# Layer 0's experts in fours, chosen and added by one-hot matmuls on the chip

## The reference

```python
for i in range(DEPTH):                      # 2 layers
    h = h + mixer_i(rmsnorm(h))             # attention, then chunked gMLP
    h = h + hier_moe(rmsnorm(h))            # 32 experts, 1024 -> 2 x 256 -> 1024
    h = h + sigmoid(rmsnorm(h) @ W_g) * (p[i] @ W_p)   # "ple"

h1 = einsum('td,edf->tef', t, w_gate); h2 = einsum('td,edf->tef', t, w_up)
a = silu(h1) * h2 * gates[:, :, None]       # gates: zero except 2 experts a token
y = einsum('tef,efd->td', a, w_down)
```

## Time and profile before

| what | us |
|---|---|
| median of 3 runs (lowest, highest) | 1098.43 (1094.73, 1100.7) |
| span of the profiled execution | 1095.3 |
| PE busy / DVE / ACT / POOL | 1021.0 / 352.3 / 186.5 / 124.5 |
| DMA, mean over the span | 281 GB/s, 308 MB |

### The profile page before, as it was taken

How to read it: one execution, slowest core, us unless ns; L and a number is a source line. 1 busy time by engine, 2 the same in 40 slices (tenths; PEclk the granted TensorE clock), 3 DMA queues, 4 the chain that set the end, 5 groups by cost and what they waited for, 6 DMA issues and landing times.

```text
span 1095.3 us, 13338 instructions
## 1 busy us (share of the span) xinstructions
PE 1021.0 (93%) x5092; PEld 603.9 (55%) x5092; DVE 352.3 (32%) x885; ACT 186.5 (17%) x384; POOL 124.5 (11%) x170
## 2 busy tenths in 40 slices
PE   6989999999998878999999999999999999988793
PEld 5766676444443324754457777777754444433372
DVE  4556225222222103632123444220342222221254
ACT  2123213111111112221012110000211111111221
POOL 2444001111111101000000000000021111110101
PEclk9999999899999999999999999999979999999997
DMA  9947885799999997933325223335469999999811
GB/s 360 369 142 245 360 349 193 296 419 418 418 419 420 419 418 302 389 145 154 154 108 196 86 110 116 115 141 230 159 248 420 418 417 418 418 419 422 321 60 43
DMA packets 61715, 308.12 MB, mean 281 GB/s; under 512 B 13778, under 2 KB 21266, under 8 KB 29650
## 3 DMA queue, kind: packets, MB, share of 16 engines
q1 hardware_dynamic: 44064, 273.53, 62.0%
q0 software_dynamic: 14656, 25.72, 7.0%
q10 hardware_dynamic: 2930, 7.99, 2.0%
HBM read 310.23 MB, written 21.08 MB: 302 GB/s over the span
## 4 chain that ended last, share of the span: by engine, by line
PE 66%; DMA 17%; issue 7%; DVE 3%; POOLq 3%; POOL 2%; ACT 1%; SPq 0%; ACTq 0%; DVEq 0%
PE ps L1574 14%; PE ps L1754 9%; PE ps L1795 9%; DMA scr_sb<-stream 8%; PE ps L1724 8%; PE ps L1583 7%; DMA ring_sb<-stream 5%; PE ps L1484 3%; PE ps L1526 3%; PE ps L1655 2%; PE ps L1560 2%; POOLq L510 2%; DMA scr_sb<-bs 1%; POOL ring_sb L511 1%; PE ps L1730 1%
## 5 line engine op out<-in xcount | busy, mean ns | idle before, releaser
L1574 PE MATMUL ps<-ring_sb,scr_sb 128*64 128x512 f32 x624 | 162.9, 611 | 14.9 <-DMA ring_sb<-stream 13.2
L1574 PEld LDWEIGHTS ps<-ring_sb,scr_sb 128*64 128x64 f32 x624 | 52.0, 141 | 119.6 <-issue 119.6
L1574 PE MATMUL ps<-scr_sb 128*64 128x512 f32 x320 | 108.6, 604 | 5.2 <-DMA scr_sb<-stream 5.2
L1583 PE MATMUL ps<-ring_sb,scr_sb 128*64 128x512 f32 x432 | 99.3, 597 | 1.1 <-ACT scr_sb L671 0.9
L1754 PE MATMUL ps<-hn_sb,ring_sb 128*128 128x288 f32 x384 | 97.9, 411 | 0.0
L1795 PE MATMUL ps<-scr_sb,ring_sb 128*128 128x288 f32 x384 | 95.2, 407 | 0.0
L1075 DVE SCALAR_TENSOR_TENSOR scr_sb<-ps,scr_sb 128x256 f32<-128x256 f32 x32 | 15.5, 484 | 243.1 <-ACT scr_sb L667 243.1
L1724 PE MATMUL ps<-ring_sb,hn_sb 128*128 128x512 f32 x192 | 83.3, 593 | 0.0
L1795 PEld LDWEIGHTS ps<-scr_sb,ring_sb 128*128 128x128 f32 x384 | 72.2, 190 | 19.3
L1754 PEld LDWEIGHTS ps<-hn_sb,ring_sb 128*128 128x128 f32 x384 | 71.5, 190 | 19.3 <-issue 0.4
L1655 PE MATMUL ps<-scr_sb,ring_sb 128*128 128x288 f32 x256 | 64.3, 406 | 0.0
(11 more groups left out here) (288 smaller groups left out, 1246.6 us busy)
## 6 DMA issues: line engine op xcount, KB each, us to landing
ring_sb<-stream SPq DMA_DIRECT2D x188, 1024.0 KB, 16.7
scr_sb<-stream SPq DMA_DIRECT2D x50, 1024.0 KB, 22.2
hn_sb<-stream SPq DMA_DIRECT2D x10, 1024.0 KB, 23.4
ring_sb<-row_pages POOLq DMA_DIRECT2D x64, 128.0 KB, 5.1
scr_sb<-key_pages SPq DMA_DIRECT2D x24, 192.0 KB, 8.9
ring_sb<-key_pages SPq DMA_DIRECT2D x24, 192.0 KB, 5.9
scr_sb<-y_rows POOLq DMA_DIRECT2D x8, 512.0 KB, 5.4
hn_rows<-scr_sb ACTq DMA_DIRECT2D x4, 512.0 KB, 3.2
```

The source lines that it names most:

```text
L1574: last = mm(ps[64 * a:64 * a + 64, 2 + b, :], xT[:, k, 64 * a:64 * a + 64], slot(a + 2 * (k // 4))[:, (k % 4) * 512:(k % 4) * 512 + 512], ...
L1583: last = mm(ps[64 * a:64 * a + 64, 5 + n, :], aT[:, k, 64 * a:64 * a + 64], slot(4 + k)[:, a * D + n * 512:a * D + n * 512 + 512], start=( ...
```

## The change

Layer 1 keeps its scheme. In layer 0:

- Experts go in 8 groups of four ("quads") of 12 slots each, with 32 places an expert (`W0`). Gate, up and down use four column tiles of 32.
- The rows of normalised h stay in SBUF (`q_hn`, scaled by ACT). `units` on DVE builds 0/1 matrices from places, and `gather_in` (24 matmuls of 128 columns) selects a quad's inputs, already turned. `gated` builds the same matrices times the gates, `turn_gated` turns them, and `add_in` (8 matmuls of 288 columns) gives the quad's contribution, which DVE adds to h at once. No row of layer 0's experts goes through HBM.
- The selection of quad n+1 stands behind the additions of quad n. The last quad's additions take the place of `combine`.
- The stream has 12 ring and 8 side positions for the first 60 expert slots, and the 12 ring positions for the rest. The ple projection is slot 80, computed in quad 5. SP's waits of layer 0 are others: slot 22 waits for the heads' value projections, slot 31 for the rows' turning, none for a gather or a read-back.
- The mixing masks are loaded by SP ahead of quad 7 and summed in it. `bs` and `b_v` come ahead of slot 113.
- If an expert of layer 0 has more than 32 tokens, a branch runs 64 further quads, with all their weights loaded again.

```diff
+W0, QUADS = 32, NE // 4
+TAIL0 = (-(-T // W0) - 1) * QUADS
...
-S_PROJ = [12, 149]
-S_MOE = [13, 150]
+S_PROJ = [80, 149]
+S_MOE = [12, 150]
+MOE0_ROW = 13
...
+ADD_BANK = (3, 7, 2)
...
+CYCLE0 = [None, None, None, 4, 5, 6, None, None, None, None, 2, 3, 0, 1, None, None, None, None, None, 7]
...
-    for L in range(2):
-        for n in range(90):
-            if n % 18 in SIDE_AT:
-                side[S_PROJ[L] + n] = RING + SIDE_AT.index(n % 18)
+    for m in range(60):
+        if CYCLE0[m % 20] is not None:
+            side[S_MOE[0] + m] = SIDE0 + CYCLE0[m % 20]
+    for n in range(90):
+        if n % 18 in SIDE_AT:
+            side[S_PROJ[1] + n] = RING + SIDE_AT.index(n % 18)
...
-            if s == RING + ROW_POS[5]:
+            if s == S_MOE[0] + 6:
                 sp.wait_ge(sem("rows_free"), 8)
-            for L in range(2):
-                if s == S_PROJ[L] + SIDE_AT[0]:
-                    if L == 0:
-                        sp.wait_ge(sem("key_free"), 8)
-                    else:
-                        sp.wait_ge(sem("g_sb"), FT)
-                        sp.wait_ge(sem("vs_ps"), 1)
-                if s == S_PROJ[L] + SIDE_AT[3]:
-                    sp.wait_ge(sem("hn_rows"), 48 * (L + 1))
-                if s == S_PROJ[L] + SIDE_AT[5]:
-                    sp.wait_ge(sem(f"member{L}"), 1)
-                    sp.wait_ge(sem("rank_ps"), 2 * L + 2)
-                    sp.wait_ge(sem(f"x_got{L}_0"), 16)
-                if s == S_GATE[L]:
-                    sp.wait_ge(sem("y12_in1"), 32 * (L + 1))
-                    sp.wait_ge(sem("y12_in2"), 32 * (L + 1))
+            if s == S_MOE[0] + 10:
+                sp.wait_ge(sem("o_ps"), H)
+            if s == S_MOE[0] + 19:
+                sp.wait_ge(sem("hr_ps"), 2)
+            if s == q_slot(QUADS - 1, 0):
+                sp.wait_ge(sem("slot_free"), q_slot(4, 5) + 1)
+                for name, dst in (("ws", wsT), ("wss", wsS)):
+                    sp.dma_start(dst, io[name]).then_inc(sem("ws_in"), 16)
+            if s == S_SGU:
+                sp.dma_start(bs, io["bs"]).then_inc(sem("bs_in"), 16)
+                sp.wait_ge(sem("h_part"), 16)
+                sp.dma_start(b_bc, io["b_v"]).then_inc(sem("bs_in"), 16)
...
+            def quad(n):
+                act.wait_ge(sem("e_h_ps"), n + 1)
+                nc.scalar.activation(q_sil, ps[:, 2, 0:FH], ACT.Silu).then_inc(sem("e_sil"), 1)
+                if n == 5:
+                    for m in range(KD):
+                        copy_prj(m)
+                act.wait_ge(sem("e_aT_ps"), n + 1)
+                nc.scalar.activation(q_aT.rearrange("p k s -> p (k s)"), ps[:, 4, 0:256], ACT.Copy).then_inc(sem("e_aT"), 1)
+                act.wait_ge(sem("e_oh_ps"), n + 1)
+                nc.scalar.activation(q_oh, bank(7, T), ACT.Copy).then_inc(sem("e_oh"), 1)
+                act.wait_ge(sem("e_y_ps"), 2 * n + 1)
+                nc.scalar.activation(q_y[:, 0:512], bank(5), ACT.Copy).then_inc(sem("q_y0"), 1)
+                if n < QUADS - 2:
+                    act.wait_ge(sem("e_x_ps"), n + 2)
+                    copy_x()
...
+            def unit_tile(n, t):
+                tn = TOK[t][1]
+                link(nc.vector.tensor_scalar(q_m01[0:tn, t, :], nat[0:tn], q_rows[0:tn, n, t:t + 1], None, ALU.is_equal))
+                return nc.vector.scalar_tensor_tensor(out=q_m01[0:tn, t, :], in0=nat[0:tn], scalar=q_rows[0:tn, n, 3 + t:4 + t],
+                                                      in1=q_m01[0:tn, t, :], op0=ALU.is_equal, op1=ALU.add)
+            def gated_tiles(rows):
+                for q in range(6):
+                    ins = nc.vector.tensor_scalar(q_mg[:, q, :], nat, rows[:, q:q + 1], tv[:, q // 3, q % 3, 2:3],
+                                                  ALU.is_equal, ALU.mult)
+                return ins
...
+            units(0)
+            gates(0)
+            for n in range(1, QUADS):
+                ins = nc.vector.tensor_scalar(q_rows[:, n, :], q_rows[:, 0, :], -float(P * n), None, ALU.add)
+            link(ins)
+            gated(0)
+            copy_x(0)
...
+            for n in range(QUADS - 1):
+                times_up(n)
+                copy_y(n)
+                for m in range(KD):
+                    dve.wait_ge(sem("q_hp"), 8 * n + m + 1)
+                    nc.vector.tensor_tensor(h_t[:, m, :], h_t[:, m, :], bank(ADD_BANK[m % 3], T), ALU.add).then_inc(sem("q_hq"), 1)
+                dve.wait_ge(sem("q_hq"), 8 * n + 8)
+                if n < QUADS - 2:
+                    copy_x(n + 1)
+                    gated(n + 1)
+                if n < QUADS - 3:
+                    units(n + 2)
...
+        def gather_in():
+            for t, (t0, tn) in enumerate(TOK):
+                for k in range(KD):
+                    last = mm(ps[:, k // 4, (k % 4) * P:(k % 4) * P + P], q_hn[0:tn, t, k * P:(k + 1) * P], q_m01[0:tn, t, :],
+                              start=(t == 0 and k % 4 == 0), stop=(t == 2 and k % 4 == 3))
+                    if t == 0 and k == 0:
+                        free_with(last)
+            return last
+        def up_part(k, w):
+            for a in range(4):
+                last = mm(ps[32 * a:32 * a + 32, 2, :], q_x[:, k, 32 * a:32 * a + 32], w[:, 512 * a:512 * a + 512],
+                          start=(k == 0), stop=(k == KD - 1))
+                if a == 0:
+                    free_with(last)
+            return last
+        def turn_act():
+            for k in range(2):
+                last = nc.tensor.transpose(ps[:, 4, k * P:(k + 1) * P], q_sil[:, k * P:(k + 1) * P], ident)
+                if k == 0:
+                    free_with(last)
+            return last
+        def turn_gated():
+            for t, (t0, tn) in enumerate(TOK):
+                mm(ps[:, 7, t0:t0 + tn], q_mg[0:tn, t, :], ident[0:tn, 0:tn], start=(t == 0), stop=False, is_transpose=True)
+            for t, (t0, tn) in enumerate(TOK):
+                last = mm(ps[:, 7, t0:t0 + tn], q_mg[0:tn, 3 + t, :], ident[0:tn, 0:tn], start=False, stop=(t == 2), is_transpose=True)
+            return last
+        def down_part(half, k, w):
+            for a in range(4):
+                last = mm(ps[32 * a:32 * a + 32, 5 + half, :], q_aT[:, k, 32 * a:32 * a + 32], w[:, 512 * a:512 * a + 512],
+                          start=(k == 0), stop=(k == 1))
+                if a == 0:
+                    free_with(last)
+            return last
+        def add_in(m):
+            return mm(bank(ADD_BANK[m % 3], T), q_y[:, m * P:(m + 1) * P], q_oh, start=True, stop=True)
...
+            route_part(0)
+            keep_busy(3, 6)
+            rank_part(0)
+            keep_busy(3, 2)
...
+            gather(0)
+            for n in range(QUADS - 1):
+                up(n)
+                if n == 5:
+                    project()
+                down(n)
+                for m in range(KD):
+                    add_y(n, m)
+                    if m >= 3:
+                        pe.wait_ge(sem("q_hq"), 8 * n + m - 2)
+                    add_in(m).then_inc(sem("q_hp"), 1)
+                if n < QUADS - 2:
+                    gather(n + 1)
...
+            n = QUADS - 1
+            gather(n)
+            up(n)
+            pe.wait_ge(sem("ws_rs"), 2)
+            for g in range(8):
+                mm(ps[:, g // 4, (g % 4) * P:(g % 4) * P + P], ones, wsT[:, g, :], start=True, stop=True)
+            for g in range(8):
+                last = mm(ps[:, 3, 32 * g:32 * g + 32], ones[0:NS_, :], wsS[0:NS_, g, :], start=True, stop=True)
+            last.then_inc(sem("rs_es_ps"), 1)
+            down(n)
+            pe.wait_ge(sem("ws_rs"), 4)
+            def combine(m):
+                add_y(n, m)
+                if m >= 3:
+                    pe.wait_ge(sem("h_upd"), 8 * H_STAGE["ple0"] + m - 2)
+                add_in(m).then_inc(sem("h_part"), 1)
+            ple_part(0, combine)
```

More of the change, by code:

```diff
@@ L102 @@
 SLOT_AT = place_slots()
+USES0 = [sum(pos == SIDE0 + n for pos, _, _ in SLOT_AT) for n in range(2)]
 def build(nc, io):
@@ L168, in program @@
     snew = A.take(NS_)
+    sm = A.take(32)
     keys = A.take(2 * 4 * 2 * 384).rearrange("p (u b g n) -> p u b g n", u=2, b=4, g=2)
@@ L357, in load_slot @@
             n = 512 if s == S_QB + 2 else SLOT
-            sp.dma_start(ring(s, 0, n), stream[s][:, 0:n]).then_inc(full(s)[0], 16)
+            sp.dma_start(ring(s, 0, n), stream[stream_row(s)][:, 0:n]).then_inc(full(s)[0], 16)
         sp.dma_start(h_t[:, :, :], io["x"]).then_inc(sem("x_in"), 16)
@@ new lines, in places, with places_beyond @@
+            link(nc.vector.tensor_scalar(over, rk, float(win), 1e5, ALU.is_ge, ALU.mult))
+            link(nc.vector.tensor_tensor(at, rk, row0, ALU.add))
+            link(nc.vector.tensor_tensor(at, at, over, ALU.add))
+        def places_beyond(win, row0, rk, over, at):
+            link(nc.vector.tensor_scalar(over, rk, float(win), float(win * NE - win), ALU.is_ge, ALU.mult))
```

(11 more changed lines are left out.)

702 lines of the change are left out of this document (486 added, 216 removed).

## The result

| what | before | after |
|---|---|---|
| median, us (lowest to highest, 4 runs each) | 1099.47 (1094.73 to 1100.7) | 1061.54 (1059.9 to 1065.68) |
| span of the profiled execution, us | 1095.3 | 1059.8 |
| first v unit of the SGU, us | 471.06 | 437.16 |

What follows compares the result with a forecast made beforehand. Layer 0's expert stage was taken as bound by transfers, ending at slot 108's landing plus what follows. 12.5 + 10.9 + 3.4 + 5.4 + 7.4 = 39.6 us off 1098.4 gave 1058.8, said as 1060; forecast range 1053 to 1066, wider range 1052 to 1081.

Steps and rivals of the forecast that it cites:

- the allowance that I had put on the sum: Whole kernel: the sum gave 1058.8 us, but 1060 was forecast because errors of the period can only cost.
- landing to down's end: End of layer 0's experts: down ends 0.9 us behind slot 108's landing instead of 4.3, 3.4 us less.
- The restart: Layer 0's stream, stopped until quad 0 releases a slot: slot 32 lands at 198.9, 12.5 us earlier.
- The rate: Slots 32 to 108: without POOL's traffic 2.50 us a slot plus masks, 191.6 us in all, 10.9 less.
- The period: PE's time for one quad in layer 0: 24.15 us, against 30 us of transfers for twelve slots.
- rival B: Quads' gate/up: four 512-column tiles go two by two, a quad 10.1 us longer, kernel 1139 us; chance 0.05.
- Its stated break-even: Quad period from which tiles going two by two would decide: 29.2 us, 5.0 over the forecast's, a step of 1.30.
- The partial overlap that I had priced at 1081: Quads' gate/up: four tiles reach 77% of full overlap, a step of 1.12 us, kernel 1081 us; chance 0.07.
- the later one decides, by one microsecond: Quad 7's end: PE's own work gives 390.3 us, transfers 391.4; the later sets the stage's end.
- The ending: Down to first v unit: 5.4 us less without scatter and read-back, 7.4 less with DVE pacing eight blocks.
- rival C: SGU or layer 1 held by transfers gives the gain back: 1080 us if half lost, 1098 if all; chance 0.04.
- D: Layer 0's window of 32 overflows and 64 further quads of 12 slots cost 1920 us; chance 0.01.

Runs made afterwards that it cites:

- experiment 2: Changed kernel with slots 30 and 31 held back until quad 0 has released its first slot: 1066.95 us.
- experiment 9: The changed kernel again, no edit, on another group's chip: median 1063.08 us over 7 runs.
- experiment 5: Changed kernel plus nine POOL transfers of 0.487 MB to an unread HBM buffer beside quads 0 to 7, without the old waits: 1074.3 us.
- experiment 6: Changed kernel with gate/up of each quad going over the eight slots twice, two column tiles at a time instead of four: 1097.82 us, one run.
- experiment 4: Changed kernel with six useless 128x512 matmuls ahead of the selection in each of quads 1 to 7: 1100.51 us, ratio 1.002 to the kernel before.
- the first execution: The changed kernel's first profiled execution, no edit: span 1059.8 us.
- experiment 8: Changed kernel with the branch for experts over 32 tokens moved on all engines from ahead of quad 7 to ahead of quad 5: 1058.59 us.
- the second execution: The profiled execution of experiment 9, the unedited changed kernel and the fastest of its runs: span 1057.4 us.
- experiment 3: Changed kernel with two useless 128x512 matmuls ahead of the selection in each of quads 1 to 7: 1071.67 us.

## Why the prediction was right, and where it was not

Predicted 1060 us, measured 1061.54, and the mechanisms of three of the four terms are there. That the number is so near is in part luck: the terms add up to 39.6 us, and the profiles show 33.9. Of the 5.7 too many, 1.6 came back behind the v unit, 1.2 was the allowance that I had put on the sum, and 1.4 came from the medians: they lie 4.2 and 1.7 us above the two profiles, and a fourth run raised the one before by 1.0. The terms, as "earlier than before":

| term | predicted | measured | from |
|---|---|---|---|
| slot 32's landing | 12.5 | 11.3 | 211.4 to 200.1 |
| 32 to 108 | 10.9 | 8.5 | 202.5 to 194.0 |
| landing to down's end | 3.4 | -0.6 | 4.3 to 4.9 |
| down to first v unit | 5.4 + 7.4 | 14.7 | 52.8 to 38.1 |
| sum | 39.6 | 33.9 | 471.06 to 437.16 |

**The restart** was right in mechanism (experiment 2). Selection began at 185.60 (said: 186.1) and ran at the high level, but gate/up of quad 0 took 8.84 us in place of 7.14, at low clock from its first step on. Quad 0 started 0.9 us sooner than I had said (192.17, not 193.1), and still slot 32 was issued 1.2 later (195.2, not 194.0). I had counted 0.9 us from the quad's start to that issue. It takes 1.9 at the high level (experiment 9: 192.4 to 194.4) and took 3.0 here at the low one.

**The rate.** POOL's traffic was priced rightly (experiment 5). The remaining stream took 2.53 us a slot and not 2.50: (194.0 - 1.6)/76.

**PE's own time.** The period was right to 0.6 us, and rival B, the pairs, did not come: experiment 6 had to be built to see it. Its stated break-even is 0.9 us too low (experiment 4). The partial overlap that I had priced at 1081 did not come either: 0.89 us for four tiles against 0.859 for a pair is nearly full overlap. The Trainium skill, in "TensorE: Matmul & The Clock Gate", section "Measured speedup vs the span model", reports less for such packing (3.07 times for four row tiles, 2.38 times for three column tiles); here the measurement differs from it and decides.

**The step that failed** is "the later one decides, by one microsecond", the comparison of PE's own end (390.3) with the transfers' (391.4). In the first execution PE's end less its waits for stream is 399.0 - 5.1 = 393.9, in the second 394.1 - 3.7 = 390.4, so the sums were near. But a wait in quad 5 or 6 isn't given back in quad 7. There the branch, the units, the sums of the masks and the low clock stand behind slot 96, and PE's 37.6 us from there (361.4 to 399.0) are longer than the 33.6 that the last twelve slots and a step take. I had the branch and units at 3 us; they took 6.2 in one execution and 3.6 in another, plus 1.4 to 2.3 of low clock in the selection behind and 1.4 to 1.8 in down. In the first execution this one step cost 4.0 us (4.9 behind the landing, not 0.9), and in experiment 8, which moves the branch to where PE has lead, down ends 3.4 sooner. In the second execution, with the short gap, PE takes 34.2 us from slot 96 (359.9 to 394.1), and the step cost 0.6 us (1.5, not 0.9); against that one experiment 8's down ends 1.5 later. So the order of the two ends was wrong both times, by a size that changes from execution to execution, and moving the branch removes the long gap but gains nothing on an execution that had the short one.

**The ending** gave 1.9 us more than predicted: the blocks follow one another every 1.26 us on DVE, not 1.36 (the first two even after 0.80 and 1.02), and y's second half takes 0.69, not 0.85. That the shortening of the ending comes from the rows no longer going through HBM and from the smaller blocks is read from the two traces; no run tried it by itself.

**The rest.** SGU and layer 1 take 622.6 us from the first v unit, 624.2 before, both within the scatter of 621.5 to 625.5: rival C (the gain given back) is out. D did not occur.

## What to carry to other kernels

Where a ring feeds one engine from a stream, compare the two not once, at the end, but at every landing: the end is the latest of (landing + what the engine still has to do behind it). A wait in the middle plus a serial stretch at the end is longer than either total. Put branches, drains and side sums where the engine would wait anyway, and count every queue's bytes at the stream's price.

## What the runs showed of the hardware

- Four 32-column tiles at 512 fp32 columns take 0.87 to 0.89 us, two take 0.86: the overlap is nearly full, and where two passes over the slots meet, pairs of both overlap too (experiment 6: 12.25 us for 16 pair steps, not 13.8).
- Writes of 3.90 MB on POOL's queue, beside a stream at 419 GB/s, put off that stream by 9.3 us, 2.4 us per MB: as much as their bytes of the stream itself.
- A stretch at the low clock (0.50) begins right behind a selection and its 0.85 us of waiting, in two of the eight quads of the changed kernel (0 and 2 in one execution, 5 and 6 in the other) and in six of experiments 3 and 4, with busy matmuls ahead of the selection; it costs 1.5 to 1.7 us of gate/up each time.
- Ahead of quad 7, at a branch that isn't taken, PE stands still for 3.6 us (until DVE's last unit) or for 6.2 to 7.6 (beyond it), in two executions of the same code for 3.6 and 6.2. With the low clock, and with the 4 us of scatter behind the first v unit, this may well be the spread of the runs, 1059.3 to 1065.7 us over eleven of the changed kernel; only two of these were profiled.
